# Ten of the first eleven weight chunks of the second block's input product in plain fp32, and an earlier, denser schedule for its scan and its recurrence

## The chip, the cores and the metric

One core of one Trainium2 chip. The metric is the device time in microseconds (us) of one execution; lower is better. The kernel before takes 1556.94 us, the median of three runs (1555.85 to 1557.4).

## The reference

Two transformer blocks of width 1024 over 256 tokens, in fp32. The change is in the second one, whose input product feeds three branches and their gates:

```python
h = rmsnorm_2(x, norm_mix[l])
proj = h @ w_in[l]
fq, fk, fv, ff, su, hq, hf, hi, hg, gl = jnp.split(proj, split_pts, axis=-1)
...
y_fox = fox_attention(q, k, v, log_f)
y_s5 = s5_mixer(su, ...)
y_hg = hgrn2_mixer(hq, hf, hi, hg, lb_all[l], hg_onorm[l])
gates = jax.nn.sigmoid(gl)
merged = gates[:, :, 0] * (y_fox @ wb[:512]) + gates[:, :, 1] * (y_s5 @ wb[512:1024]) + gates[:, :, 2] * (y_hg @ wb[1024:])
```

`s5_mixer` is a complex linear scan over time for 32 groups of 64 states (16 tiles of 128 rows in the kernel). `hgrn2_mixer` is a gated linear recurrence with four heads; it takes silu(hq) as its query and is gated at its end by silu(hg).

## The kernel before

**Products and chunks.** The weights stream from HBM in chunks of 1 MB into a ring of seven slots. A chunk holds four tiles of 128 rows by 512 columns; a group of 512 output columns of the input product (`in2`) needs two chunks. TensorE works on a chunk in four parts, here called **quarters** (one tile of 128 rows each), and the schedule of everything beside the product counts in quarters. `in2` has 29 chunks: group 0 is chunks 0 and 2, chunk 1 is the narrow one (the forget gate's eight columns), and group g is chunks 2g+1 and 2g+2 from there on. Chunk e is quarters 4e to 4e+3. The groups come in this order: su (0, the scan's input), the recurrence's forget logits (1) and queries (2, with a silu), its values (3), fq, fk and fv (4 to 6), the recurrence's output gate hg (7, with a silu, chunks 15 and 16), and six groups of branch gates.

**Split and plain chunks.** A split chunk is multiplied in three passes of fp32r: ACT rounds it (`split_hi`, line 1372), DVE forms the remainder in place (`split_lo`, line 1386), and PE multiplies high by high, low by high and high by low (lines 1058 and 1066). A plain chunk is read by PE from the ring as fp32 (`plain_chunk`, lines 1093 and 1096) and costs ACT and DVE nothing. `PLAIN` names the plain chunks of a product; before, they are 0, 2, 4, 6, 8 and 10 of `in2`. The split of chunk e+2 stands in the programs of ACT and DVE at the third and the fourth quarter of chunk e.

**Guests.** The other branches are woven between the quarters. Each guest is a list of steps for every engine, and `paced([(n0, n1, q0, q1)])` spreads steps n0 to n1 evenly over quarters q0 to q1. The order on each engine is thus fixed by hand: work of quarter q, then the steps due at q, in program order; semaphores make the engines wait for each other.

- The scan (`S5`, line 3120) has 21 steps. The first, on DVE, waits until the last store of kept rows to HBM has landed (`kept_at(3)`, the DMA of line 664), since it then clears a buffer that lies over them (lines 3234 and 3240). On ACT it computes the first sine and cosine tables. Step n, for n from 2, is loop index i = n-2. PE gives at even i the drives of tiles i and i+1 (line 3154), and at odd i from 3 the outputs of tiles i-3 and i-2 (line 3170), which wait for what DVE turned out at index i-1 (line 3276). DVE does at index i turn in (lines 3250, 3252), scan (3267), add (3258) and turn out (3274, 3276), some with a 128x256 sum (3289); even indices wait for the drive.
- `HgrnPrep` (line 3297): three steps, logarithms on ACT, sums over time on DVE.
- The recurrence (`Hgrn`, line 3338) has 21 steps: two that clear buffers, then 17 of one kind, in which DVE forms arguments (3440, 3441), ACT takes their exponential (3411), DVE multiplies the operands (3459, 3461), PE multiplies them (3382), and DVE takes the product (3483).
- The forget gate's guest, `ForgetGate`, has its last step on DVE at quarter 12, as before.

DVE and ACT copy a finished group out of its PSUM banks at the start of the next chunk's work. For groups 2 and 7 ACT uses silu, and the second half waits for DVE's copy:

```python
if i == 7:
    act.wait_ge(k.dve_took, k.dve_groups[first + 8])
    st(act.activation(hg[:, 1, :], hg[:, 1, :], ACT.Silu))
```

Of the kernel before, what the change touches and what calls it, by code (L numbers as in the profile page):

```python
# [95 lines left out]
    ("swi_down", "w_down_2", 0, FF2T, groups("tok", 0, D)),  # L96
]
MEM_AT = {"up0": 0, "in1": 1, "up1": 2, "in2": 3}
PLAIN = {"in2": (0, 2, 4, 6, 8, 10)}
GUESTS = {"in0": [-1, -1, 0, 1, 10, 12, 14, 16, 18], "out0": [5],  # L100
          "up0": [1, 3, 5, 7, 9, 11], "down0": [1, 4, 7, 10, 13],
          "out1": [3], "up1": [3, 9]}
# [851 lines left out]
class Product(Stage):  # L954
# [9 lines left out]
    def __init__(self, k, name, src, act_out, dve_out, act_after=None, dve_after=None, is_split=False,  # L964
# [19 lines left out]
        for kind, i, j, _ in stream_of(name):  # L984
# [11 lines left out]
            else:  # L996
                if len(self.own) in PLAIN.get(name, ()):
                    k.plain.add(len(k.split_chunk))
# [30 lines left out]
    def tensor(self, pe):  # L1029
# [3 lines left out]
        for e, (c, i, j) in enumerate(self.own):  # L1033
# [15 lines left out]
            for kk in range(nk):  # L1049
                f = k0 + kk  # L1050
                if i == 0 or self.name in PLAIN:
                    self.wait_source(pe, f)
# [408 lines left out]
def paced(parts, to_the_end=False):  # L1461


    def due(q):
        if q is None:
            return None if to_the_end else parts[-1][1]
        n = parts[0][0]
        for n0, n1, q0, q1 in parts:
            if q > q0:
                n = n0 + -(-(n1 - n0) * min(q - q0, q1 - q0) // (q1 - q0))  # L1470
        return n
    return due
# [2239 lines left out]
def in2_stage(k, fqk, fv, suT, hqT, fT, hi, hg, gl, join):  # L3712
    first = k.groups + 1

    def q_act(act, st, i, bank):
        return act.activation(hqT[:, 0:2, :], bank.rearrange("p (a b) -> p a b", a=2), ACT.Silu)

    def q_dve(dve, st, i, bank):
        return dve.tensor_copy(hqT[:, 2:4, :], bank.rearrange("p (a b) -> p a b", a=2))

    def hg_act(act, st, i, bank):
        return act.activation(hg[:, 0, :], bank, ACT.Silu)

    def hg_dve(dve, st, i, bank):
        return dve.tensor_copy(hg[:, 1, :], bank)

    def act_after(act, st, i):
        if i == 2:
            act.wait_ge(k.dve_took, k.dve_groups[first + 3])
            st(act.activation(hqT[:, 2:4, :], hqT[:, 2:4, :], ACT.Silu))  # L3730
# [4 lines that stand above are left out]
    outs = by_ranges((1, to_features(suT)), (1, to_features(fT)), (1, (q_act, q_dve)), (1, to_rows(hi)),  # L3735
                     (2, to_rows(fqk)), (1, to_rows(fv)), (1, (hg_act, hg_dve)),
                     *((2, to_rows(gl[:, :, n * D:(n + 1) * D])) for n in (2, 1, 0)))
    return Product(k, "in2", Operand(None, k.h_hi, k.h_lo, join.made, join.full, join.full_made), *outs, act_after, None, lead=(join,))
# [524 lines left out]
def block2_stages(k, base, small, keep, s5, post):  # L4263
# [48 lines left out]
    in2 = in2_stage(k, fqk, fv, suT, hqT, fT, hi, hg, gl, join)  # L4312
    join.follow(in2)
    gate = ForgetGate(k, tmp, negc, in2)
    s5_stage = S5(k, suT, bT, mag, turns, cs, n, r, cos, sn, ab, g, h, b2, z, first, gate)
    s5_stage.after = keep
    hg_prep = HgrnPrep(k, fT, key, b, htmp, first)
    hgrn = Hgrn(k, hqT, hg_prep, hi, ho, arg, qs, ks, acc, first, s5_stage)
# [36 lines left out]
    def glu_act_after(act, st, i):  # L4355
# [42 lines left out]
    later = lambda parts: [(n0, n1, q0 + a, q0 + b) for n0, n1, a, b in parts]  # L4398
    return [
        Woven(k, Chain(k, in2, glu, hg_out, s5_out, fox_out, mix_out, queries, xo, gate_up, swi_down),  # L4400
              (Threaded(gate), paced([(0, 3, 8, 14)])), (Threaded(s5_stage), paced([(0, 21, 12, 70)])),
              (Threaded(hg_prep), paced([(0, 1, 56, 57), (1, 3, 57, 66)])),
              (Threaded(hgrn), paced([(0, 21, 70, 94)])),
              (Threaded(hg_norm), paced([(0, 1, 97, 98), (1, 2, 103, 104), (2, 3, 107, 108), (3, 4, 108, 109)])),
              (Threaded(prep), paced([(0, 3, 94, 101), (3, 4, 101, 102), (4, 6, 109, 111)])),
              (Threaded(glu_split), paced([(0, 1, 109, 110)])),
# [14 lines left out]
def all_stages(k, bias, kept, kept_hi):  # L4421
# [93 lines left out]
                                  [(Threaded(prep), paced([(0, 10, 72, 120)], True))],  # L4515
                                  lambda: [prep.m["taken"].at(2)])
    return stages + layer1 + block2_stages(k, 192, small, mem, s5, down1)


# [122 lines left out]
```

## Time and profile before

| | before |
|---|---|
| median of three runs | 1556.94 us |
| the profiled execution, its own time | 1556.36 us |
| span of that execution, first to last instruction | 1554.6 us |
| mean granted TensorE clock (1 is full) | 0.984 |
| PE busy | 1468.7 us, 94% of the span |
| DVE busy | 1127.4 us, 73% |
| ACT busy | 780.7 us, 50% |
| POOL busy | 70.6 us, 5% |

In the chain that ended last PE has 48%, PE's weight loads 15%, DVE 20% and ACT 7%. `in2` itself begins at 949.3 us of the span. A timeline line gives start, duration, engine, line of the code, operation, operands, shape and count of the merged instructions, and in brackets how long the engine had been idle before and who ended that. Durations of successive matmuls overlap; what an instruction costs is read from its start to the next one's start. A plain fp32 matmul appears as two records.

### The profile page before, as it was taken

What the parts mean: (1) busy time and instruction counts of PE and PEld (TensorE: products, weight loads), DVE (VectorE), ACT (ScalarE), POOL (GpSimd) and SP (SyncE); (2) the same over time, 40 slices, a digit from 0 to 9 for tenths busy, and PEclk for the clock granted to TensorE, in tenths of its full rate; (3) what the DMA queues carried; (4) which work ended last, traced back from release to release, by engine and by line L of the source; (5) the groups of instructions that cost most, each with busy time, mean ns of one, the idle gap of its engine ahead of it and who ended that gap; (6) DMA issues with size and microseconds to landing.
All of it is one profiled execution on the core that took longest, in us unless ns stands there. A gap on an engine that the chain in (4) does not pass through costs nothing.

```text
span 1554.6 us, 22128 instructions
## 1 busy us (share of the span) xinstructions
PE 1468.7 (94%) x8815; PEld 1257.2 (81%) x8818; DVE 1127.4 (73%) x1818; ACT 780.7 (50%) x1073; POOL 70.6 (5%) x82
## 2 busy tenths in 40 slices
PE   5789989999999999999999999999999899999998
PEld 5788766799988889877899888756776578799987
DVE  6798876699776757766886556999985665566653
ACT  4766655454534645454555435557454634354442
POOL 0000000000000000000000003820020000000000
PEclk8999999999999999999999999999999999999999
DMA  9757623589677544336566555323344243245551
GB/s 388 298 203 274 241 102 129 216 328 363 253 315 297 187 153 142 130 136 241 179 247 238 179 214 193 136 109 136 109 140 159 82 163 109 109 163 189 186 190 59
DMA packets 42517, 298.56 MB, mean 192 GB/s; under 512 B 4656, under 2 KB 4912, under 8 KB 7472
## 3 DMA queue, kind: packets, MB, share of 16 engines
q1 hardware_dynamic: 39984, 283.52, 48.9%
q0 software_dynamic: 1568, 8.39, 1.5%
q10 hardware_dynamic: 864, 5.24, 0.9%
q8 instruction: 71, 1.16, 0.3%
q14 instruction: 30, 0.25, 0.0%
HBM read 292.94 MB, written 4.19 MB: 191 GB/s over the span
## 4 chain that ended last, share of the span: by engine, by line
PE 48%; DVE 20%; PEld 15%; ACT 7%; issue 7%; DMA 2%; PEldq 1%; ACTq 0%; SPq 0%; DVEq 0%
PE ps L1058 20%; PE ps L1066 14%; PEld ps L1058 8%; PEld ps L1066 6%; DVE ring_at_lo L1386 6%; ACT w_hi L1372 3%; DVE ring_at L1235 2%; DMA ring_at<-stream 2%; PE ps L1121 2%; PE ps L2700 1%; DVE arena_at L2268 1%; PE ps L1096 1%; DVE arena_at L3267 1%; PE ps L3611 1%; PE ps L3170 1%
## 5 line engine op out<-in xcount | busy, mean ns | idle before, releaser
L1386 DVE TENSOR_TENSOR ring_at_lo<-ring_at,w_hi 128x2048 fp32r<-128x2048 f32 (+1 forms) x212 | 481.6, 2274 | 158.9 <-ACT w_hi L1372 158.1
L1372 ACT ACTIVATE w_hi<-ring_at 128x2048 fp32r<-128x2048 f32 (+1 forms) x212 | 400.9, 1898 | 176.7 <-PE ps L1058 121.1
L1058 PE MATMUL ps<-w_hi,arena_at_lo 128*128 128x512 f32 x1104 | 300.5, 394 | 1.6 <-DVEq L4563 0.8
L1066 PE MATMUL ps<-h_hi,w_hi 128*128 128x256 f32 x1376 | 228.8, 288 | 15.0 <-DVE ring_at_lo L1386 12.0
L1058 PEld LDWEIGHTS ps<-w_hi,arena_at_lo 128*128 128x128 f32 x1104 | 204.4, 188 | 46.0 <-issue 2.7
L1066 PE MATMUL ps<-hT_at_lo,w_hi 128*128 128x256 f32 x1376 | 219.9, 282 | 0.0
L1066 PE MATMUL ps<-h_hi,ring_at_lo 128*128 128x256 f32 x1376 | 219.8, 282 | 0.0
L1066 PEld LDWEIGHTS ps<-h_hi,w_hi 128*128 128x128 f32 x1376 | 190.9, 191 | 22.2 <-issue 13.8
L1066 PEld LDWEIGHTS ps<-h_hi,ring_at_lo 128*128 128x128 f32 x1376 | 188.7, 190 | 0.0
L1066 PEld LDWEIGHTS ps<-hT_at_lo,w_hi 128*128 128x128 f32 x1376 | 188.4, 190 | 0.0
L1058 PE MATMUL ps<-ring_at_lo,arena_at_lo 128*128 128x512 f32 x552 | 170.4, 390 | 0.0
L1058 PEld LDWEIGHTS ps<-ring_at_lo,arena_at_lo 128*128 128x128 f32 x552 | 103.7, 188 | 22.3
L1235 DVE CUSTOM_DVE_ANT_0 ring_at<-ring_at,arena_at 128x1024 f32<-128x1024 f32 x96 | 114.5, 1219 | 7.6 <-DMA ring_at<-stream 7.6
L1058 PE MATMUL ps<-w_hi,h_hi 128*128 128x512 f32 x352 | 119.2, 420 | 0.0
L1058 PE MATMUL ps<-w_hi,hT_at_lo 128*128 128x512 f32 x352 | 111.4, 398 | 0.0
L1058 PE MATMUL ps<-ring_at_lo,h_hi 128*128 128x512 f32 x352 | 111.1, 397 | 0.0
L1058 PEld LDWEIGHTS ps<-w_hi,hT_at_lo 128*128 128x128 f32 x352 | 66.7, 190 | 16.1
L1058 PEld LDWEIGHTS ps<-ring_at_lo,h_hi 128*128 128x128 f32 x352 | 66.6, 189 | 16.2
L1058 PEld LDWEIGHTS ps<-w_hi,h_hi 128*128 128x128 f32 x352 | 63.5, 191 | 17.3 <-issue 6.1
L1121 PE MATMUL ps<-w_hi,arena_at_lo 128*128 128x512 f32 x128 | 35.1, 396 | 3.0 <-DVEq L4563 2.0
L1721 ACT ACTIVATE arena_at_lo<-arena_at 128x1024 fp32r<-128x1024 f32 x16 | 17.0, 1061 | 40.0 <-DVE arena_at L1808 40.0
L3836 ACT ACTIVATE arena_at<-arena_at 128x512 f32<-128x512 f32 x11 | 7.0, 632 | 52.2 <-DVE arena_at L3824 52.2
(468 smaller groups left out, 1711.8 us busy)
## 6 DMA issues: line engine op xcount, KB each, us to landing
ring_at<-stream SPq DMA_DIRECT2D x266, 1024.0 KB, 4.9
arena_at_lo<-kept_hi POOLq DMA_DIRECT2D x4, 1024.0 KB, 7.1
arena_at<-bias ACTq DMA_DIRECT2D x4, 768.0 KB, 6.4
kept<-arena_at POOLq DMA_DIRECT2D x4, 512.0 KB, 4.7
arena_at<-kept ACTq DMA_DIRECT2D x2, 1024.0 KB, 5.8
x_res<-x SPq DMA_DIRECT2D x1, 1024.0 KB, 10.3
arena_at<-mem POOLq DMA_DIRECT2D x1, 1024.0 KB, 13.3
kept_hi<-arena_at_lo POOLq DMA_DIRECT2D x1, 1024.0 KB, 5.2
```

Of the source, the lines that this page charges most:

```text
L1058: mm = pe.matmul(k.ps[:, bank + t, :], x_tile(f, slice(t * P, (t + 1) * P)), w, start=first and n == 0, stop=last and n == 2)
L1066: mm = pe.matmul(k.ps[:, bank + q // 2, (q % 2) * TOK:(q % 2 + 1) * TOK], w[:, q * P:(q + 1) * P], x, start=first and n == 0 and q % 2 == ...
L1096: mm = pe.matmul(k.ps[:, bank + q // 2, (q % 2) * TOK:(q % 2 + 1) * TOK], w[:, q * P:(q + 1) * P], src.full[:, f, :], start=first and q % ...
L1121: mm = pe.matmul(k.ps[:, bank + t, :], x[:, f, t * P:(t + 1) * P], w, start=f == 0 and n == 0, stop=f == KD - 1 and n == 2)
L1235: dve.tensor_tensor_reduce(w, w, k.cond_row, 1.0, 0.0, ALU.mult, ALU.add, self.guest.column(n, q)) \
L1372: act.activation(k.w_hi[:, r % HI, 0:n, :], k.ring[:, c % RING, 0:n, :], ACT.Identity).then_inc(k.hi_done, 1)
L1386: dve.tensor_tensor(k.w_lo[:, c % RING, 0:n, :], k.ring[:, c % RING, 0:n, :], k.w_hi[:, r % HI, 0:n, :].bitcast(F32), ALU.subtract).then_i ...
L1721: act.activation(self.uo.hi[:, at, :], self.uo.f[:, at, :], ACT.Identity).then_inc(self.m["hidden_hi"].sem, 1)
L2268: ins = dve.scalar_tensor_tensor(self.xc[:, j, :], src, w, self.xc[:, j, :], ALU.mult, ALU.add)
L2700: mm = pe.matmul(k.ps[:, 6 + t, 0:MDV + 2], a, b, start=j == 0, stop=j == len(parts) - 1)
L3170: mm = pe.matmul(k.ps[rows, 6 + q % 2, 0:TOK], self.cs[:, c, e, :], part[:, e % 3, c * TOK:(c + 1) * TOK], start=n + c == 0, stop=n + c == 2)
L3267: dve.tensor_tensor_scan(self.g[:, at], mag, a[:, at], 0.0, ALU.mult, ALU.add) \
```

## The change

Four more chunks of `in2` are plain: 3, 5, 7 and 9, so that now chunks 0 and 2 to 10 are. The scan's 21 steps are spread over quarters 10 to 60 in place of 12 to 70, the recurrence's preparation over 50 to 60 in place of 56 to 66, and the recurrence's 21 steps over quarters 62 to 94 in place of 70 to 94. The norm behind the recurrence and everything later keep their quarters.

```diff
-PLAIN = {"in2": (0, 2, 4, 6, 8, 10)}
+PLAIN = {"in2": (0, 2, 3, 4, 5, 6, 7, 8, 9, 10)}
...
-              (Threaded(gate), paced([(0, 3, 8, 14)])), (Threaded(s5_stage), paced([(0, 21, 12, 70)])),
-              (Threaded(hg_prep), paced([(0, 1, 56, 57), (1, 3, 57, 66)])),
-              (Threaded(hgrn), paced([(0, 21, 70, 94)])),
+              (Threaded(gate), paced([(0, 3, 8, 14)])), (Threaded(s5_stage), paced([(0, 21, 10, 60)])),
+              (Threaded(hg_prep), paced([(0, 1, 50, 51), (1, 3, 51, 60)])),
+              (Threaded(hgrn), paced([(0, 21, 62, 94)])),
```

## Rows read from the trace of the kernel before

**Rows 1.** windows: PE, PEld, DVE, ACT, POOL busy, clock, DMA share, GB/s; two stretches
```profile
1047.40:1053.90 6.50, 3.63 (x18) 1.30 (x16) 6.50 (x12) 2.56 (x6) 0.00 (x0) 0.74 0.00 0
...
1090.80:1138.60 47.80, 44.71 (x259) 37.74 (x259) 45.63 (x88) 20.88 (x26) 0.00 (x0) 1.00 0.31 109
```

**Rows 2.** waits of PE from 930 to 1260: total us, times, longest us
```profile
PE ps L3170 <- DVE arena_at L3276: 5.4, 5, 2.9
...
PE ps L3382 <- DVE arena_at L3461: 2.9, 3, 1.5
```

**Rows 3.** timeline of PE: start, us, count; plain chunks and a split one
```profile
959.02 7.07 PE L1096 MATMUL ps<-arena_at,ring_at 128*128 128x256 f32 x32
965.74 0.82 PE L1066 MATMUL ps<-h_hi,w_hi 128*128 128x256 f32 x4
966.40 0.63 PE L1066 MATMUL ps<-hT_at_lo,w_hi 128*128 128x256 f32 x4
...
967.34 0.63 PE L1066 MATMUL ps<-h_hi,w_hi 128*128 128x256 f32 x4
...
1025.96 5.42 PE L1093 MATMUL ps<-ring_at,arena_at 128*128 128x512 f32 x12
1031.31 1.13 PE L3154 MATMUL ps<-arena_at 32*128 32x256 f32 x8
```

**Rows 4.** timeline of PE around products of the scan, the longest wait last
```profile
993.52 1.13 PE L3154 MATMUL ps<-arena_at 32*128 32x256 f32 x8
994.59 3.72 PE L1096 MATMUL ps<-arena_at,ring_at 128*128 128x256 f32 x16
...
999.78 1.92 PE L3170 MATMUL ps<-arena_at 128*32 128x256 f32 x16
1001.63 0.73 PE L1058 MATMUL ps<-w_hi,h_hi 128*128 128x512 f32 x2
...
1050.50 3.54 PE L3170 MATMUL ps<-arena_at 128*32 128x256 f32 x16 [2.87 <-DVE arena_at L3276]
```

**Rows 5.** timeline of DVE: start of a scan step and of what follows it, twice
```profile
982.91 0.67 DVE L3250 TENSOR_TENSOR arena_at<-ps,arena_at 128x512 f32<-128x512 f32 x1
...
987.80 2.48 DVE L1386 TENSOR_TENSOR ring_at_lo<-ring_at,w_hi 128x2048 fp32r<-128x2048 f32 x1
...
1050.37 0.68 DVE L3250 TENSOR_TENSOR arena_at<-ps,arena_at 128x512 f32<-128x512 f32 x1
...
1054.54 2.28 DVE L1386 TENSOR_TENSOR ring_at_lo<-ring_at,w_hi 128x2048 fp32r<-128x2048 f32 x1
```

**Rows 6.** timeline of POOL: the last store of the kept rows is issued
```profile
956.25 0.69 POOL L664 DMA_DIRECT2D kept<-arena_at  x1 [35.80 <-DVE arena_at L1139]
```

**Rows 7.** DMA issues from 930 to 1060: size and us to landing of that store
```profile
kept<-arena_at POOLq DMA_DIRECT2D x1, 512.0 KB, 9.9
```

**Rows 8.** source view of line 664: from issue to landing, all four stores
```profile
DMA to landing us min/median/max: 3.1/4.7/9.9
```

**Rows 9.** timeline of DVE where the scan begins
```profile
966.12 0.69 DVE L1750 COPY arena_at<-ps 128x512 f32<-128x512 f32 x1 [6.43 <-PE ps L1096]
...
969.12 0.91 DVE L3234 MEMSET arena_at<- 128x1024 f32 x1 [0.16 <-issue]
...
972.25 0.69 DVE L3250 TENSOR_TENSOR arena_at<-ps,arena_at 128x512 f32<-128x512 f32 x1
```

**Rows 10.** timeline of ACT: second half of the gate, then the exponential's table
```profile
1085.33 0.62 ACT L3733 ACTIVATE arena_at<-arena_at 128x512 f32<-128x512 f32 x1
...
1087.77 1.28 ACT L3411 ACT_TABLE_LOAD   x1
```

**Rows 11.** timeline of PE: first products of the recurrence
```profile
1092.35 1.13 PE L3382 MATMUL ps<-arena_at 128*128 128x128 f32 x8 [1.49 <-DVE arena_at L3461]
...
1094.72 1.06 PE L3382 MATMUL ps<-arena_at 128*128 128x128 f32 x8
1095.54 0.71 PE L1058 MATMUL ps<-w_hi,h_hi 128*128 128x512 f32 x2
```

## The prediction

> **What bounds the kernel now.** I read the busy shares and the chain of waits of the page first: PE carries most of the chain. Then the waits of PE from 930 to 1260 us, since the change lies in the input product, from 949.3 to about 1166 us. PE waits there for DVE: 5.4 us in five waits before outputs of the scan and 2.9 us in three before products of the recurrence [rows 2]. After the longest, 2.87 us, the next product of the scan takes 3.54 us where one without a wait takes 1.92 [rows 4]; the granted clock of that stretch is 0.74 [rows 1]. I call this a dip and put it at 3.54 less 1.92, about 1.6 us. So what waiting costs here is 5.4 + 1.6 + 2.9 = 9.9 us; that is all that relief of DVE could return. In the recurrence DVE is busy 45.63 of 47.80 us [rows 1], in step with PE. The timelines give the unit costs below, each from one start to the next.
>
> **The work of PE.** A plain feature chunk takes 6.72 us (959.02 to 965.74). Of a split one a pass over a quarter takes 0.47 (966.40 to 967.34 are two), so the chunk 12 x 0.47 = 5.6. Twelve records of a plain token chunk take 5.35 us, so all sixteen 7.13; a split one is again 5.6 [rows 3]. Chunks 3 and 5 are feature chunks, 7 and 9 token chunks: 2 x 1.1 + 2 x 1.5 = **+5.2 us**. Against it stand seams: the first pass after a plain chunk takes 0.66 (965.74 to 966.40) and not 0.47 [rows 3]. Four such seams go (0.8 us). About ten drives and outputs of the scan, fp32 themselves, stood in split chunks and come to stand in plain ones or later ones; each seam in and out was some 0.2 us together (2.0 us). Work: 5.2 - 2.8 = **+2.4 us**. Bounds: +5.2 if no seam counts, +1.5 if each costs a little more.
>
> **What DVE and ACT lose.** Four splits go, 2.2 us each on DVE (the one at 1054.54 has 2.28) [rows 5]: about 9 us less to do. What counts is whether PE's waits fall, and for that the new spacing has to be laid out.
>
> **The start of the scan.** Step 1 moves from quarter 12 to quarter 10, and so ahead of DVE's copy of group 0, which stands at quarter 12. Step 1 waits for the landing of the last store of kept rows. This store is issued at 956.25 [rows 6] and lands 9.9 us later [rows 7], at 966.15. Before, that was over when DVE came to step 1 at 969.12 [rows 9]. Now DVE waits till 966.15, clears and fills for 3.13 us (969.12 to 972.25), and only then copies group 0, which it did at 966.12 before [rows 9]: the copy ends at about 969.9. The first drive needs that copy. PE will have done quarter 12 at 965.74 + 1.68 = 967.42 [rows 3] and wait till about 970.0: a **new wait of 2.6 us**. Behind step 1 on DVE are queued the copy, the last step of the forget gate and the first turn in, so DVE starts the scan at the same 972.25 as before. The queue of POOL isn't changed, and the store is issued ahead of all that moves. Bounds: nothing, if the store lands as the quickest of the four does, after 3.1 us [rows 8]; 2.6 if it lands as here. I take 2.6, its own row.
>
> **The spacing of the scan.** From `paced`, the quarters between a pair of drives and the next outputs were always three up to index 15. In the change they are 2, 3, 3, 2, 2, 3, 3 for drives at 17, 21, 26, 31, 36, 40, 45. Between the two PE needs 1.07 for the drive (993.52 to 994.59) and the quarters; DVE needs the drive, then a step of 4.17 us (1050.37 to 1054.54), or of 4.89 (982.91 to 987.80) while POOL computes phases [rows 4, 5]; with 0.2 for the handshakes DVE is ready 5.4 to 6.2 us after the drive began. Two plain quarters and the drive are 2 x 1.68 + 1.07 = 4.4, or 4.6 with token quarters. So PE waits 1.75 at the first, 1.5 at the fourth and 1.2 at the fifth (the steps there being 4.9, 4.9 and 4.6, the last with a sum). Three plain quarters are 6.1 to 6.4: no wait, but 0.45 at the third, which has a sum too. At index 15 three split quarters give 0.4. The last outputs (quarter 52) come behind a split, a whole step and a scan on DVE: 1.2. With the start: 2.6 + 1.75 + 0.45 + 1.5 + 1.2 + 0.4 + 1.2 = 9.1 us, in place of 5.4 and the dip of 1.6: **+2.1 us**. DVE does less and PE waits more, since it is the latency from drive to output that is short of quarters, not DVE's throughput. Bounds: 0 waits if DVE had its results always ready (-7.0), and 12 if each of seven took 1.7 (+5.0).
>
> **The recurrence.** Its 17 products begin at quarter 65 and not 72, in 1.5 quarters each and not 1.14. DVE comes to them with the sums over time, the gelu of the scan's output ahead of ACT's rounding, two clears and three splits behind it; I find it ready about as late after PE as before: 1.5 us for the 1.49 [rows 11]. Of the other two waits, 1.4 in all, 0.5 stay, since PE now has 1.5 x 1.41 + 0.82 (1094.72 to 1095.54, [rows 11]) = 2.9 us for a step of DVE.
> But group 7 is copied at quarter 68, with silu on ACT, and this was before the first exponential and now falls between the second and the third. Before, silu came at 1085.33 and the load of the exponential's table at 1087.77, 1.28 us, in a gap in which ACT had nothing else to do for PE [rows 10]. Now: PE ends quarter 67 at T. DVE copies to T+0.9, ACT's second half goes to T+1.5 (0.62, [rows 10]), the table to T+2.8, the exponential to T+3.4, DVE's operands to T+4.2, PE can multiply at T+4.3. PE has done quarter 68 at T+1.4: a **new wait of 2.9 to 3.1 us**. The load of silu's own table can be done ahead. Behind the waiting exponential, on ACT, stand the later ones; behind DVE's operands its arguments, its take and the split. Bounds: 1.6 if no load is needed after silu, 4 if silu's load comes late as well. I take 3.0. Sum: 1.5 + 0.5 + 3.0 = 5.0 for 2.9: **+2.1 us**.
> The Trainium skill, "ScalarE: Activation LUTs", section "What ACT_TABLE_LOAD costs", adds a drain of some 1.4 us to each load of about 1.28; by it this wait would be 4.4 us and the whole 1.4 us more. In the row before, the load alone takes 1.28 and nothing of a drain can be seen, as ACT then waited for other engines.
>
> **Behind quarter 94** nothing moves. The next long wait of PE, for the norm, comes after a copy for which DVE waits on PE, so an earlier or later recurrence is carried through as a mere shift. What I cost at nothing: the preparation of the recurrence on ACT (quarters 50 and 51), hidden as its results are needed by DVE at 55; and the DMA of the ring, whose slots come free as before.
>
> **Sum.** 2.4 + 2.1 + 2.1 = **+6.6 us** against the profiled execution's own 1556.36 (span 1554.6): 1563.0. The median of the runs is 0.6 above it, so 1556.94 + 6.6 = **1563.5 us**. I count no new dip; each would add 1.6.
>
> **Rivals.**
> 1. *The store lands early.* DVE does step 1 in its idle 6.43 us [rows 9]. No wait of 2.6: 1561. Against it: the row of this very store. 0.12.
> 2. *No load behind silu, or the waits overlap with ones I counted.* The recurrence gives +0.5: 1562, and with rival 1 1559. For it: I can't see exponential and then silu in these rows. 0.15.
> 3. *Dips.* Two new waits of 2.6 and 3 us are near the 2.87 that was followed by one: 1565 to 1567. 0.18.
> 4. *Faster: DVE is what bounds.* If DVE's step, rid of 9 us of splits, is ready when two plain quarters are over, all waits of the scan go (-7.0), and the recurrence loses two of its three (-1.4); with work of +2.4 that is 1551. It decides at a latency from drive to output under 4.5 us; the rows give 5.4 at least. 0.10.
> 5. *The edits cancel.* A bit of 4 with the new waits halved: 1558. 0.15. That chunks aren't plain after all can't be: `PLAIN` is read by number, and 0 to 10 without 1 are those named.
>
> **How the numbers follow.** The forecast 0.30, 1563.5, its own range 1561 to 1565. What a measurement of this kernel can tell from no change is 0.2%, 3.1 us: 1553.8 to 1560.1. Faster: rival 4 for the most, 0.10. Same: rival 5, and the low part of rivals 1 and 2, 0.25. Slower: 0.65. The range takes in 3 and the lower part of 2 and 5: 1556.5 to 1568.
>
> **What would show it.** Right: a wait of PE of about 2.6 us before the first drive, with DVE's clear ahead of its copy of group 0; waits of 1 to 2 us before three or four outputs of the scan in plain chunks; one table load more on ACT between the second and third exponentials, and a wait of 3 us before PE's third product of the recurrence; plain chunks of 6.7 and 7.1 us. Wrong: a landing before 963 us; PE's waits for line 3276 below 3 us in all; the recurrence without a wait over 2 us.

## The result, and the profile after

The changed kernel takes 1563.18 us (median of 6 runs, 1561.03 to 1565.17), the kernel before 1556.56 us beside it (6 runs). The ratio is 1.0036, 95% interval 1.0020 to 1.0052: slower by 5.6 us, 3.1 to 8.1 (the plain difference of the two medians is 6.6). The forecast was 1563.5. The profiled execution took 1562.98 us, its span is 1561.2.

The page, busy time by engine (us, share of the span, instructions):

```profile
PE 1475.5 (95%) x8767; PEld 1257.3 (81%) x8770; DVE 1117.7 (72%) x1814; ACT 773.8 (50%) x1070; POOL 60.3 (4%) x82
```

Against the table of before PE has 6.8 us more to do, DVE 9.7 and ACT 6.9 less: the four splits went, as costed. What that relief is worth shows only in PE's waits.

The waits of PE from 930 to 1260 us, in answer to [rows 2] (total, number, longest):

```profile
PE ps L3170 <- DVE arena_at L3276: 6.0, 5, 1.9
...
PE ps L3382 <- DVE arena_at L3461: 2.9, 1, 2.9
...
PE ps L3154 <- issue: 1.0, 1, 1.0
```

The timeline of PE from the start of the scan to its last output (start, duration, engine, line, tiles, count, idle time before), in answer to [rows 3] and [rows 4]:

```profile
959.35 8.80 PE L1096 MATMUL ps<-arena_at,ring_at 128*128 128x256 f32 x40
969.14 1.13 PE L3154 MATMUL ps<-arena_at 32*128 32x256 f32 x8 [0.99 <-issue]
970.20 8.90 PE L1096 MATMUL ps<-arena_at,ring_at 128*128 128x256 f32 x40
979.03 1.13 PE L3154 MATMUL ps<-arena_at 32*128 32x256 f32 x8
...
985.71 1.92 PE L3170 MATMUL ps<-arena_at 128*32 128x256 f32 x16 [1.90 <-DVE arena_at L3276]
...
992.27 5.45 PE L1096 MATMUL ps<-arena_at,ring_at 128*128 128x256 f32 x24
997.65 1.92 PE L3170 MATMUL ps<-arena_at 128*32 128x256 f32 x16
...
1009.57 1.92 PE L3170 MATMUL ps<-arena_at 128*32 128x256 f32 x16
...
1021.02 1.92 PE L3170 MATMUL ps<-arena_at 128*32 128x256 f32 x16 [1.20 <-DVE arena_at L3276]
...
1034.18 1.92 PE L3170 MATMUL ps<-arena_at 128*32 128x256 f32 x16 [1.20 <-DVE arena_at L3276]
...
1046.07 1.92 PE L3170 MATMUL ps<-arena_at 128*32 128x256 f32 x16
...
1056.87 1.92 PE L3170 MATMUL ps<-arena_at 128*32 128x256 f32 x16 [0.44 <-DVE arena_at L3276]
...
1065.85 1.92 PE L3170 MATMUL ps<-arena_at 128*32 128x256 f32 x16 [1.26 <-DVE arena_at L3276]
...
1086.01 1.05 PE L3382 MATMUL ps<-arena_at 128*128 128x128 f32 x8
...
1095.04 2.05 PE L3382 MATMUL ps<-arena_at 128*128 128x128 f32 x8 [2.88 <-DVE arena_at L3461]
1096.74 1.20 PE L1058 MATMUL ps<-w_hi,h_hi 128*128 128x512 f32 x2
1097.74 0.71 PE L1058 MATMUL ps<-w_hi,hT_at_lo 128*128 128x512 f32 x2
```

Waits before the eight outputs: 1.90, 0, 0, 1.20, 1.20, 0, 0.44, 1.26. They follow the gaps of two and three quarters as laid out in the forecast (1.75, 0, 0.45, 1.5, 1.2, 0, 0.4 and 1.2). The recurrence's first two products wait for nothing, the third 2.88 us, and then a pass of two records takes 1.00 us from start to start (1096.74 to 1097.74), where the next one takes 0.54 (to 1098.28): a dip. The windows around it give its clock (columns as in [rows 1]):

```profile
1095.00:1098.40 3.40, 3.36 (x13) 3.12 (x14) 3.12 (x7) 1.94 (x2) 0.00 (x0) 0.57 0.00 0
1098.40:1102.00 3.60, 3.60 (x22) 3.05 (x21) 3.60 (x7) 0.63 (x1) 0.00 (x0) 1.00 0.02 5
```

What stood behind the 2.88 us, on ACT and then on DVE, in answer to [rows 10]:

```profile
1086.46 1.28 ACT L3722 ACT_TABLE_LOAD   x1
1090.80 0.60 ACT L3722 ACTIVATE arena_at<-ps 128x512 f32<-128x512 f32 x1 [3.06 <-PE ps L1058]
1091.52 0.63 ACT L3733 ACTIVATE arena_at<-arena_at 128x512 f32<-128x512 f32 x1
1092.17 1.28 ACT L3411 ACT_TABLE_LOAD   x1
1093.47 1.15 ACT L3411 ACTIVATE arena_at<-arena_at 128x512 f32<-128x512 f32 x2
...
1090.80 0.69 DVE L3725 COPY arena_at<-ps 128x512 f32<-128x512 f32 x1 [0.77 <-PE ps L1058]
...
1094.13 0.43 DVE L3459 TENSOR_TENSOR arena_at<-arena_at 128x256 f32<-128x256 f32 x1 [1.97 <-ACT arena_at L3411]
```

Silu's table is loaded ahead (1086.46). Silu waits for PE's group 7, its second half for DVE's copy; only then come the load of the exponential's table, 1.28 us, and the exponential that the third product needs. That is the forecast's chain.

And the start of the scan on DVE, in answer to [rows 9], with the store's landing, in answer to [rows 7]:

```profile
965.54 0.91 DVE L3234 MEMSET arena_at<- 128x1024 f32 x1 [5.52 <-DMA kept<-arena_at]
...
968.34 0.69 DVE L1750 COPY arena_at<-ps 128x512 f32<-128x512 f32 x1
...
kept<-arena_at POOLq DMA_DIRECT2D x1, 512.0 KB, 8.7
```

The clear stands ahead of the copy of group 0 and waits 5.52 us for the store, as forecast, but the store landed in 8.7 us and not 9.9.

### The profile page after: what moved, and what is told of

The parts are those of the page before. It is cut to its first block, busy times and chain, and to the rows that moved or that the text cites. A ratio compares the mean times of both kernels' runs of the same rounds, so it can differ in the third digit from the quotient of the medians.

```text
span 1561.2 us, 22021 instructions
## 1 busy us (share of the span) xinstructions
PE 1475.5 (95%) x8767; PEld 1257.3 (81%) x8770; DVE 1117.7 (72%) x1814; ACT 773.8 (50%) x1070; POOL 60.3 (4%) x82
## 3 DMA queue, kind: packets, MB, share of 16 engines
q8 instruction: 71, 1.16, 0.3%
## 4 chain that ended last, share of the span: by engine, by line
PE 54%; DVE 17%; PEld 15%; ACT 6%; issue 5%; DMA 2%; PEldq 1%; ACTq 0%; SPq 0%; DVEq 0%
PE ps L1058 22%; PE ps L1066 14%; PEld ps L1058 8%; PEld ps L1066 6%; DVE ring_at_lo L1386 5%; PE ps L1096 2%; ACT w_hi L1372 2%; DVE ring_at L1235 2%; DMA ring_at<-stream 2%; PE ps L1121 2%; PE ps L1093 1%; PE ps L2700 1%; PE ps L3382 1%; DVE arena_at L2268 1%; PE ps L3170 1%
## 5 line engine op out<-in xcount | busy, mean ns | idle before, releaser
L1386 DVE TENSOR_TENSOR ring_at_lo<-ring_at,w_hi 128x2048 fp32r<-128x2048 f32 (+1 forms) x208 | 472.5, 2274 | 158.4 <-ACT w_hi L1372 157.7
L1372 ACT ACTIVATE w_hi<-ring_at 128x2048 fp32r<-128x2048 f32 (+1 forms) x208 | 393.4, 1898 | 172.1 <-PE ps L1058 115.1
L1066 PE MATMUL ps<-h_hi,w_hi 128*128 128x256 f32 x1344 | 222.9, 288 | 14.4 <-DVE ring_at_lo L1386 11.6
L1066 PE MATMUL ps<-h_hi,ring_at_lo 128*128 128x256 f32 x1344 | 214.3, 281 | 0.0
L1066 PE MATMUL ps<-hT_at_lo,w_hi 128*128 128x256 f32 x1344 | 214.3, 281 | 0.0
L1066 PEld LDWEIGHTS ps<-hT_at_lo,w_hi 128*128 128x128 f32 x1344 | 183.5, 190 | 0.0
L1058 PE MATMUL ps<-w_hi,h_hi 128*128 128x512 f32 x336 | 112.7, 417 | 0.0
L1058 PE MATMUL ps<-ring_at_lo,h_hi 128*128 128x512 f32 x336 | 106.1, 397 | 0.0
L1096 PE MATMUL ps<-arena_at,ring_at 128*128 128x256 f32 x192 | 43.4, 382 | 0.0
L1096 PEld LDWEIGHTS ps<-arena_at,ring_at 128*128 128x128 f32 x192 | 35.9, 190 | 6.8 <-issue 2.1
```

Source lines behind the costliest of these rows:

```text
L1058: mm = pe.matmul(k.ps[:, bank + t, :], x_tile(f, slice(t * P, (t + 1) * P)), w, start=first and n == 0, stop=last and n == 2)
L1066: mm = pe.matmul(k.ps[:, bank + q // 2, (q % 2) * TOK:(q % 2 + 1) * TOK], w[:, q * P:(q + 1) * P], x, start=first and n == 0 and q % 2 == ...
L1096: mm = pe.matmul(k.ps[:, bank + q // 2, (q % 2) * TOK:(q % 2 + 1) * TOK], w[:, q * P:(q + 1) * P], src.full[:, f, :], start=first and q % ...
L1372: act.activation(k.w_hi[:, r % HI, 0:n, :], k.ring[:, c % RING, 0:n, :], ACT.Identity).then_inc(k.hi_done, 1)
L1386: dve.tensor_tensor(k.w_lo[:, c % RING, 0:n, :], k.ring[:, c % RING, 0:n, :], k.w_hi[:, r % HI, 0:n, :].bitcast(F32), ALU.subtract).then_i ...
```

## How the runs are read

A run's time scatters by some 5 us to either side, more than most edits here are worth. So next to the ratio stands a measure from the one profiled execution: **the stretch**, from the first product of `in2` to the norm's first product (line 3880). It is 216.66 us before (949.29 to 1165.95) and 221.94 after (949.62 to 1171.56): +5.28, beside +5.6 by the ratio. From the stretch I take the waits that PE shows in it for the scan and the recurrence, and the dips, each as the excess of the starts of its instructions over the same ones at full clock (in after 0.89 + 0.44 + 0.08 = 1.4). What is left, against before's, is **the rest**: PE's work and whatever isn't a listed wait. Before: 5.42 + 2.94 + 1.62 = 10.0 us of waits and dips [rows 2, 4], so the rest of a kernel is its stretch less 216.66, plus 10.0, less its own waits and dips. For after: 5.28 + 10.0 - 11.3 = +4.0.

The stretch comes from one execution and scatters too. After, e3 and e4 don't differ before quarter 62; from the start of `in2` to the scan's last output they take 116.2, 116.6 and 117.8 us (to 1065.85, 1066.16 and 1069.79). So a difference of up to some 1.6 us between two stretches can be chance, unless the rows show the instruction that makes it.

| kernel | plain chunks | scan, recurrence over | ratio (95%) | stretch | scan waits | recurrence waits | dips | rest |
|---|---|---|---|---|---|---|---|---|
| before | 6 | 12-70, 70-94 | 1 | 216.66 | 5.4 | 2.9 | 1.6 | 0 |
| after | 10 | 10-60, 62-94 | 1.0036 (1.0020-1.0052) | 221.94 | 1.0 + 6.0 | 2.9 | 1.4 | +4.0 |
| e1 | 10 | 12-70, 70-94 | 1.0018 (1.0002-1.0033) | 219.24 | 3.3 | 2.9 | 1.6 | +4.7 |
| e2 | 6 | 10-60, 62-94 | 1.0058 (1.0038-1.0078) | 226.57 | 2.4 + 9.7 | 2.9 | 4.8 | 0.0 |
| e3 | 10 | 10-60, 70-94 | 1.0028 (1.0013-1.0043) | 221.07 | 1.2 + 6.2 | 2.3 | 0 | +4.8 |
| e4 | 10, no silu | 10-60, 62-94 | 1.0033 (1.0013-1.0053) | 220.74 | 1.9 + 5.0 | 1.5 | 1.7 | +4.1 |
| e5 | 10 | 12-65, 62-94 | 1.0005 (0.9990-1.0021) | 220.58 | 1.1 | 5.5 | 3.3 | +4.0 |
| e7 | 6 | 12-74, 70-94 | 1.0041 (1.0019-1.0062) | 225.09 | 11.5 | 2.9 | 4.3 | -0.3 |
| e8 | 10 | 12-74, 70-94 | 1.0065 (1.0043-1.0087) | 226.24 | 9.0 | 2.9 | 3.0 | +4.7 |
| e9 | 5 | 12-70, 70-94 | 0.9994 (0.9975-1.0012) | 218.06 | 7.1 | 2.9 | 2.8 | -1.4 |
| e10 | 6 | 12-65, 70-94 | 0.9986 (0.9968-1.0003) | 215.43 | 5.1 | 2.2 | 1.5 | 0.0 |
| e11 | 10 | 12-65, 70-94 | 0.9982 (0.9967-0.9996) | 214.73 | 1.1 | 2.3 | 0 | +4.7 |
| e12 | 8 | 12-65, 70-94 | 1.0011 (0.9990-1.0032) | 216.11 | 3.4 | 2.3 | 1.7 | +2.1 |
| e13 | 7 | 12-65, 70-94 | 0.9996 (0.9975-1.0017) | 214.06 | 3.9 | 2.3 | 0 | +1.2 |

Where two numbers stand under scan waits, the first is the wait before the first pair of products. Stretch and ratio agree within the intervals except for e5, whose stretch is 3.9 us longer than before's and whose ratio allows 3.3 at most; the profile of one execution can't settle that. e8's profiled execution was the slowest of its seven, 1575.81 us for a median of 1567.64; its stretch, 9.6 us longer, fits the ratio (10.1), so what it lost beyond that lies elsewhere.

The last column is the most regular one: whatever the schedule, six plain chunks give -0.3 to 0.0, five -1.4, seven +1.2, eight +2.1, ten +4.7 (+4.0 with the recurrence from 62; why it is less there, the runs don't show).

## Experiments

### Each half alone: e1 and e2

```diff
 # e1: the kernel before, with
-PLAIN = {"in2": (0, 2, 4, 6, 8, 10)}
+PLAIN = {"in2": (0, 2, 3, 4, 5, 6, 7, 8, 9, 10)}
 # e2: the kernel before, with
-paced([(0, 21, 12, 70)])   ... paced([(0, 1, 56, 57), (1, 3, 57, 66)])   ... paced([(0, 21, 70, 94)])
+paced([(0, 21, 10, 60)])   ... paced([(0, 1, 50, 51), (1, 3, 51, 60)])   ... paced([(0, 21, 62, 94)])
```

> The ten plain chunks with the schedule of before (scan 12 to 70, recurrence 70 to 94). Theory (the new schedule costs, the plain chunks cost only PE's work): PE's work grows by some 4 to 5 us, and as every pair of drive and output keeps three quarters, the waits before outputs of the scan fall from 5.4 us to 2 or less and the dip of 1.6 goes; the recurrence keeps its 2.9. Together -2 to +1 us against before, and 5 to 8 us below the changed kernel. Rival (the plain chunks are the loss): +4 to +6 against before, as the changed kernel.

> The new schedule with the old set of plain chunks. Theory: the outputs that follow their drives by two split quarters (2.8 us and the drive's 1.1) find DVE 1.5 us or more late, and DVE has its four splits of 2.2 us beside: waits before outputs of the scan 12 us or more, the wait of 2.9 us with its dip at the third product of the recurrence as in the changed kernel; +7 to +14 us against before. Rival (the schedule is neutral and the plain chunks are the loss): within 2 us of before.

e1 is 2.8 us slower (0.3 to 5.1), e2 9.0 us (5.9 to 12.1). Each half costs time, e1 by an amount only just clear of zero, and together they cost less (5.6) than their sum: the plain chunks relieve DVE of splits and thereby lower the waits that the tight schedule makes, from 12.1 us to 7.0 at the scan. In e1 only two of the five waits of [rows 2] are left, and one is the old 2.87 us. Its row, and DVE's ahead of it:

```profile
1054.00 3.56 PE L3170 MATMUL ps<-arena_at 128*32 128x256 f32 x16 [2.88 <-DVE arena_at L3276]
...
1043.33 0.68 DVE L3250 TENSOR_TENSOR arena_at<-ps,arena_at 128x512 f32<-128x512 f32 x1
...
1047.49 2.29 DVE L1386 TENSOR_TENSOR ring_at_lo<-ring_at,w_hi 128x2048 fp32r<-128x2048 f32 x1
1049.69 0.69 DVE L3250 TENSOR_TENSOR arena_at<-ps,arena_at 128x512 f32<-128x512 f32 x1
```

Between the turn in of 1043.33 and that of 1049.69, which the output waits for, DVE works off the split of 1047.49. Four plain chunks more don't touch it, since it is a split of a chunk behind the eleventh.

e2's waits by line, and the window with its longest dip (PE at 0.50, the 1.2 GHz level):

```profile
PE ps L3170 <- DVE arena_at L3276: 9.7, 7, 3.5
...
PE ps L3154 <- issue: 2.4, 1, 2.4
...
1020.00:1024.00 4.00, 3.18 (x16) 1.29 (x16) 4.00 (x7) 1.95 (x5) 0.22 (x1) 0.50 0.00 0
```

### The recurrence: e3 later, e4 without silu

```diff
 # e3: the changed kernel, with
-paced([(0, 21, 62, 94)])
+paced([(0, 21, 70, 94)])
 # e4: the changed kernel, with (group 7, both halves)
-act.activation(..., ACT.Silu)
+act.activation(..., ACT.Identity)
```

> The changed kernel with the recurrence at 70 to 94 again; silu for group 7 comes ahead of all exponentials. Theory: the wait of 2.9 us before the third product and its dip of 1.4 go; two or three waits of the denser recurrence come back, 1 to 3 us in all; 1 to 4 us below the changed kernel. Rival (the wait is DVE being late with the recurrence, not the table): a wait of about 3 us stays near the first products, same time as the changed kernel.

> The changed kernel, leaving out one part of the computation: group 7 is copied without its silu, so no other table is needed between the exponentials. Theory: the table load of 1.28 us between silu and the exponential goes; the copy's two halves stay in ACT's way, so the wait of 2.9 us before the third product falls to about 0 to 1.6 and the dip goes; 3 to 4.5 us below the changed kernel. Rival (ACT waits for DVE's copy and for PE, the table is hidden): the wait stays above 2.5 us and the time is the same.

e3: 4.4 us slower than before (2.0 to 6.7), its intervals and those of after overlap. In the trace the 2.88 us wait and the dip are gone, three of 0.7 to 0.8 us are in their place, 2.0 us less together; the stretch falls by 0.9 only, as the rest is 0.8 more. e4 leaves out the silu of the output gate, no more. The wait in question:

```profile
1097.55 1.13 PE L3382 MATMUL ps<-arena_at 128*128 128x128 f32 x8 [1.46 <-DVE arena_at L3461]
```

1.46 us for 2.88: the table between silu and the exponential is worth 1.42, beside 1.28 for the load in the row above, and the dip behind the wait goes too. From the last output of the scan to the products behind the recurrence (line 3395) e4 takes 74.27 us and after 77.04: 2.8 less, 1.4 of wait and 1.4 of dip. But e4's start wait is 1.86 and was followed by a dip:

```profile
972.38 1.13 PE L3154 MATMUL ps<-arena_at 32*128 32x256 f32 x8 [1.86 <-issue]
973.44 10.57 PE L1096 MATMUL ps<-arena_at,ring_at 128*128 128x256 f32 x40
983.94 1.13 PE L3154 MATMUL ps<-arena_at 32*128 32x256 f32 x8
```

Forty records of a plain chunk take 10.50 us there and 8.83 in after (970.20 to 979.03): 1.7 us that have nothing to do with silu. That is why its stretch is only 1.2 us shorter than after's, and its ratio (5.1 us above before, 2.0 to 8.2) can't be told from after's.

### Gaps of three: e5

```diff
 # the changed kernel, with
-paced([(0, 21, 10, 60)])
+paced([(0, 21, 12, 65)])
```

> The changed kernel with the scan's steps over quarters 12 to 65 in place of 10 to 60: every output now stands three quarters behind its pair of products (in the change three of seven stand two behind), and step 1 of the scan stands behind the copy of group 0 again. Recurrence from quarter 62 as in the change. Theory A, latency: PE's wait before the first pair (1.0 us) goes, its waits before outputs of the scan fall from 6.0 to 1 to 2 us, the stretch from the start of the input product to the norm's first product falls from 221.9 by 5 to 216.5 to 218, and the time is 0 to 2 us above the kernel before. Theory B, throughput: DVE has the same work to do by quarter 94, the waits only move (to the recurrence, which now overlaps the scan), and the stretch stays at 221 to 222.

Theory A holds for the scan: no wait before the first pair, 1.1 us before outputs for 6.0. The whole is open: the stretch (220.58) is close to what theory B said, the ratio (0.8 us above before, -1.6 to +3.3) is what theory A said. In the trace the recurrence from 62 now meets a scan that ends at 63, its first product waits 2.63 us and its third again 2.88, each followed by a dip.

```profile
1084.51 1.42 PE L3382 MATMUL ps<-arena_at 128*128 128x128 f32 x8 [2.63 <-DVE arena_at L3461]
1085.58 1.20 PE L1058 MATMUL ps<-w_hi,h_hi 128*128 128x512 f32 x2
...
1095.18 1.82 PE L3382 MATMUL ps<-arena_at 128*128 128x128 f32 x8 [2.88 <-DVE arena_at L3461]
```

So with three quarters from pair to output the scan hardly waits, and a recurrence from 62 then runs into its end.

### A wider scan: e7 and e8

```diff
 # e7: the kernel before; e8: e1; both with
-paced([(0, 21, 12, 70)])
+paced([(0, 21, 12, 74)])
```

> The kernel before with the scan's steps over quarters 12 to 74 in place of 12 to 70, all else as before, the six plain chunks too: pairs after quarter 44 then stand at quarters 44, 50 and 56, no longer at 47, where a split is ahead of DVE's step. Theory A, latency and order on DVE: the wait of 2.87 us and the dip of 1.6 behind it go, and some of the other 2.5; the stretch falls from 216.7 to 211 to 213, and the time is 4 to 5 us below the kernel before. Theory B: DVE is short of throughput, the last steps of the scan and the recurrence now crowd each other behind quarter 62, and the recurrence's waits grow by what the scan's fall: no change within 1 us.

> The ten plain chunks of the change with the scan's steps over quarters 12 to 74; preparation and recurrence as before (70 to 94). Theory A: no waits of over 1 us in the scan and no dip; against e7 it differs by the work of four plain chunks alone. If seams count as I had put it (+2.4), it is 2 to 3 us above e7; if a plain chunk costs its whole 1.2 to 1.3 us, 4.5 to 5.2 us above, which puts it at the time of the kernel before within 1 us, stretch 216 to 217.5. If plain chunks pay by relief of DVE, it is below e7.

Both theories missed this: 6.4 us slower (3.0 to 9.7) and 10.1 us (6.7 to 13.5). The 2.87 us wait of [rows 4] is gone, as A said, but the last output waits 6.46 us. DVE's and ACT's rows of e7 tell why:

```profile
1065.68 0.68 DVE L3276 TENSOR_TENSOR arena_at<-arena_at 128x512 f32<-128x512 f32 x1
1071.70 2.29 DVE L1386 TENSOR_TENSOR ring_at_lo<-ring_at,w_hi 128x2048 fp32r<-128x2048 f32 x1 [5.35 <-ACT w_hi L1372]
1073.91 0.69 DVE L3250 TENSOR_TENSOR arena_at<-ps,arena_at 128x512 f32<-128x512 f32 x1
...
1079.93 2.63 DVE L3332 TENSOR_TENSOR_SCAN arena_at<-con,arena_at 128x128 f32<-128x128 f32 x8
1082.48 1.25 DVE L3267 TENSOR_TENSOR_SCAN arena_at<-arena_at 128x256 f32<-128x256 f32 x2
...
1061.74 1.28 ACT L3313 ACT_TABLE_LOAD   x1
...
1065.06 1.28 ACT L3317 ACT_TABLE_LOAD   x1
...
1067.42 1.28 ACT L3319 ACT_TABLE_LOAD   x1
...
1069.77 1.90 ACT L1372 ACTIVATE w_hi<-ring_at 128x2048 fp32r<-128x2048 f32 x1
```

The split stands on DVE ahead of a step of the scan, and waits 5.35 us for ACT's rounding (line 1372); ACT comes to it at 1069.77, after the logarithms of the recurrence's preparation with three table loads, from 1061.74 on. Behind the split and the step, DVE's program now has the recurrence's sums over time (lines 3328 and 3332, 3.8 us from 1078.68 on) ahead of the scan's last step (1082.48), whose result the last output takes; in before they stand behind it. By the rows the split's wait, 5.35 us, and those sums, 3.8, make the 6.46 together: without the first it would be some 1.1 us, without the second some 2.7, both estimates from these rows. No run separates them. In before's stretch no split from quarter 12 on waits over 0.41 us for that rounding. What e8 against e7 was to tell holds: the four plain chunks cost 4.7 - (-0.3) = 5.0 us of rest here, not 2.4.

### One plain chunk less: e9

```diff
 # the kernel before, with
-PLAIN = {"in2": (0, 2, 4, 6, 8, 10)}
+PLAIN = {"in2": (0, 2, 4, 6, 8)}
```

> The kernel before with one plain chunk less (chunk 10, a token chunk, split again), schedule as before. Its three splits come on DVE at about quarters 35 to 39. If a plain chunk costs 1.2 to 1.3 us and DVE had room there: stretch 215.4, time 1.2 us less. If DVE bounds there: PE's waits before outputs of the scan grow by 1 to 2.5 us, stretch 216.5 to 218, time the same or 1 us more. By my count of seams in the forecast the gain would be 0.6 only.

No difference that can be measured (-3.9 to +1.9 us), the stretch 1.4 us longer. The rest falls by 1.4, and PE waits 1.7 more for the scan, 1.77 before the output at 1025.94 where it was 0.61, and the dip is 1.2 longer. By this one trace a plain chunk returns its price through DVE here; the dip's length may be chance.

### Scan to 65, recurrence from 70: e10, e11, e12, e13

```diff
 # e10: the kernel before, with
-paced([(0, 21, 12, 70)])
+paced([(0, 21, 12, 65)])
 # and besides
+PLAIN = {"in2": (0, 2, 3, 4, 5, 6, 7, 8, 9, 10)}   # e11
+PLAIN = {"in2": (0, 2, 4, 6, 7, 8, 9, 10)}         # e12
+PLAIN = {"in2": (0, 2, 3, 4, 6, 8, 10)}            # e13
```

> The kernel before, six plain chunks, with the scan's steps over quarters 12 to 65 in place of 12 to 70; preparation and recurrence as before. No pair of products of the scan then stands at quarter 47 or at 56, so that no split waiting for ACT's rounding stands on DVE between a late pair and its output. Theory A (place of the splits): the 2.87 us wait and its dip go, other waits stay near 2.5; the stretch falls from 216.7 to 212 to 213.5, the time is 3 to 4.5 us below the kernel before. Theory B (DVE short of throughput with the split chunks left in): a pair comes every 5 quarters and not every 5.8, DVE was busy 15.00 of 15 us in two stretches before; waits of 1 to 2.5 us before most outputs, 8 to 10 in all; stretch 218 to 220, time 2 to 3 us above.

> Ten plain chunks of the change, scan over quarters 12 to 65, recurrence at 70 to 94 as before. It has neither the early first pair, nor steps of two quarters, nor the silu between exponentials. Waits: 1.1 us before outputs of the scan as in the run with the scan to 65, 2.9 in the recurrence as before, no dip: 4.0 in all, against 9.9 before. With the work of four plain chunks at +4.7 to +5.2 the stretch is 215.5 to 216.5 and the time 0 to 1 us below the kernel before; with work of +2.4 as I had forecast, 213 and 3.5 us below.

> As the run before it, with chunks 7, 9 added to the six plain ones and 3, 5 split again: eight plain chunks. The work of two plain token chunks is +2.4 to +2.6 us (2.0 and 3.0 as bounds). Theory A: waits of about 4 us, stretch 213.5 to 215, the time 2 to 3 us below the kernel before, and below both its neighbours with ten and with six plain chunks. Theory B: waits of 1.2 to 2 us come back at the outputs behind quarters 12 to 24, where chunks 3 and 5 are split again, 3 to 5 us of them; stretch 217 to 219.

> Scan to quarter 65, recurrence from 70, and the six plain chunks of before with chunk 3 alone added. Chunk 3 is where the first output of the scan waited 2.26 us behind a split on DVE and was followed by a dip of 0.8; both go, the wait of 1.03 at the third output and the small ones stay: waits of 4.5 to 5 us against 8.2 (dip counted) with six plain chunks. The price by the rows is 1.2 to 1.3 us for one plain chunk: stretch 213 to 214, 1 to 2 us below both the run with six (215.4) and the one with ten (214.7); time about 4 us below the kernel before. If the wait only moves one output on (DVE short of throughput), the stretch is 215.5 to 217.

e11 is 2.8 us faster than before (0.6 to 5.1), with the very plain chunks of the change. Of the twelve variants it is the only one whose interval leaves out 1 on the fast side, and only just (0.9996). Its waits:

```profile
PE ps L3170 <- DVE arena_at L3276: 1.1, 2, 0.7
...
PE ps L3382 <- DVE arena_at L3461: 2.3, 3, 0.8
```

In e10, with six plain chunks, the wait at quarter 50 has gone and the first output waits 2.26 us in its place, followed by a dip:

```profile
989.20 2.71 PE L3170 MATMUL ps<-arena_at 128*32 128x256 f32 x16 [2.26 <-DVE arena_at L3276]
```

Both theories are half right: A on the late waits, B on the front, where DVE has splits and full steps side by side. e12, with chunks 3 and 5 split, has the same wait (2.25 us) and dip; e13, with 3 plain alone, has 0.20. In e10 DVE begins the step behind that pair 2.46 us after PE began the pair and takes 5.15 us for it, in e13 1.17 and 4.38: that is the whole difference of 2.06. So it is chunk 3 that the first output needs plain, and 5, 7 and 9 together return less than they cost: from e13 to e11 the waits fall by 2.8 and the rest rises by 3.5. By the stretch e13 is the shortest (214.06), by the ratio it can't be told from before (-3.9 to +2.6 us), nor from e11. The better of the two stays open: their stretches differ by 0.7 us, which is within the scatter, and only e11's ratio is clear of 1.

## Why the prediction was right, and where it was not

The time was forecast at 1563.5 and came out at 1563.18. The direction and most of the mechanism were right; that the two numbers are 0.3 us apart is luck. The forecast took the work of PE 1.6 us too low and the waits 2.9 us too high, and the two errors cancelled in good part.

- **The work of PE, +2.4, was mis-sized: +4.0 to +4.7.** The unit costs were nearly right (5.2 for four chunks, 4.7 to 5.0 between e1, e11, e8 and their like with six); the 2.8 us that I took off for seams weren't there. After shows it: 24 records take 5.38 us (992.27 to 997.65 above), forty 8.83 (970.20 to 979.03), that is 0.216 each and some 0.2 for each run that ends before a product of the scan. What I read as a seam between plain and split chunks is paid wherever a run of passes or records is broken, so it doesn't go when the neighbour turns plain. The stated upper bound, +5.2 if no seam counts, was nearer.
- **The start of the scan, 2.6: it was 0.99.** The mechanism is there, row for row. The store landed 1.2 us sooner after its issue, and DVE was at the copy 2.80 us after it began to clear (965.54 to 968.34), where the forecast had 3.13. The landing and the clearing behind it set it: landing and clearing took 8.7 and 2.80 us in after (wait 0.99), 9.0 and 2.65 in e3 (1.16), 9.2 and 3.13 in e4 (1.86), 9.4 and 3.28 in e2 (2.45); with step 1 behind the copy (e5, e11) there is no wait.
- **The spacing, 6.5: it was 6.0,** in the places and nearly the sizes of the forecast. The waits over 1 us stand at the gaps of two quarters and at the last output, the gaps of three have 0.44 us at the most, and with three everywhere (e5, at a pace 6% slower) 1.1 us is left: the latency from pair to output makes them. But DVE's load counts beside it: with the four splits back and the same gaps (e2) they are 9.7.
- **The recurrence, 5.0: it was 2.88 and a dip of 1.4.** The wait behind silu was forecast at 2.9 to 3.1 and is 2.88; e4 shows its cause. The first wait of 1.5 isn't there. It goes with the schedule, not with the plain chunks: 1.45 to 1.49 with a scan to 70 or 74 (before, e1, e7, e8), 0.80 with one to 60 or 65 and the recurrence from 70 (e3, e10, e11), none in after and e2, 2.63 in e5. Nor are the small ones there. The dip was in rival 3, not in the forecast.
- **Rivals.** 1 (the store lands early) is half true: it landed 1.2 us sooner, not in DVE's idle time. 2 (no load behind silu) is false: the load is there. 3 (dips) is true of one wait in two. 4 (DVE bounds, so faster) is false: DVE got 9.7 us shorter and PE waits no less, as the schedule took back what the relief gave. 5 (the edits cancel) is false: e1 and e2 are both slower.

In all I forecast +2.4 for work and +4.2 for waits; the stretch of one execution shows +4.0 and +1.3.

The Trainium skill, "ScalarE: Activation LUTs", section "What ACT_TABLE_LOAD costs", adds a drain of some 1.4 us to each load; by it the wait would have been 4.4 us, an estimate from the forecast's 3.0. The trace disagrees: silu's second half starts at 1091.52 and takes 0.63, the load starts at 1092.17 and the exponential at 1093.47, 1.30 later, and taking the load away gave back 1.42.

## What to carry to other kernels

When work is moved from a helper engine to the one that bounds, charge it its full unit price, and count as gain only waits that can be named in the trace, each with the instruction that ends it. In a schedule written out by hand, look at each helper for what stands in its program between a product and the result that the bounding engine waits for: a split that waits for another engine's rounding there, or another branch's work, can cost more than many splits elsewhere (the last output of e7). And whether such a move pays hangs on the schedule around it: ten plain chunks for six make the stretch 2.6 us longer with the old schedule (e1), 1.2 longer with the scan to 74 (e8 against e7), 0.7 shorter with the scan to 65 (e11 against e10, within the scatter) and 4.6 shorter with the change's (after against e2).

## What was not expected of the hardware

The granted clock falls to its 1.2 GHz level behind some waits of PE and not behind others of the same length. Waits of 1.90 us (after) and 1.92 (e3) before the first output left it at 1.00. Waits of 1.86 us before the first pair (e4; there from 1.1 us behind the wait on), 2.05 (e7) and 2.26 (e10) before outputs were followed by means of 0.52, 0.58 and 0.64 over the next 3 to 5 us. The norm's wait, 2.02 us in both, was followed by 0.67 in before and by 1.00 in e3. A dip cost 1.4 to 1.7 us in most places, 2.7 behind the 6.46 us of e7 and 2.8 behind the 2.88 of e9. So the length of the wait alone doesn't decide; what else does, the runs don't settle. And the store of 512 KB that took 3.1 us in the quickest of its four issues took 8.7 to 9.9 us at this place in all fourteen kernels.
